# A hybrid decoder layer in fp32r passes: the output gate's inner product as fp32r products, and copies, low parts and loads moved between engines

## The chip, the cores and the metric

The kernel runs on one core of one Trainium2 chip. The metric is the time of one execution on the device, in microseconds (us); lower is better. Everything happens in a single launch: all weights come from the chip's memory (HBM), the result is written back to it, and the intermediate results that do not fit into SBUF go through HBM as well.

## The reference

One layer for a sequence of 1024 tokens and a model width of 1024, all in float32. What bears on the change:

```python
h = rms_norm(x) * (1 + sc1) + sh1
proj = h @ w_in                       # RG-LRU, RWKV-7 and attention branches, merge gates
lru_x, lru_y, p_rw, q, k, v, gates = jnp.split(proj, IN_POINTS, axis=-1)
# RWKV-7 branch: the output gate is a low-rank product over 160 inner channels
g = jax.nn.sigmoid(gl) @ g2           # gl: (1024, 160), g2: (160, 1024)
out = (y + bonus) * g                 # y: the delta-rule state's output
o_a = (ha * gelu(lru_y)) @ w_lru_o    # RG-LRU branch, 1280 inner channels
y_c = sliding_window_attention(q, k, v, q_gain, k_gain, sinks)
mixed = (gate_a * o_a + gate_b * o_b + gate_c * o_c) @ w_out
x = x + g1 * mixed
x = x + g2 * swiglu(rms_norm(x) * (1 + sc2) + sh2, w_ffn_in, w_ffn_out)
```

## The kernel before

**Layout.** Activations stand transposed in SBUF: 128 channels on the partitions, 1024 tokens along the free dimension. A dense product takes one block of 128 output channels at a time (`dense`, which calls `three_passes`). Both operands are split into a high part in fp32r and a low part, also fp32r, which is the value less its high part. A block is then, for every 128 input channels, three passes (high·high, high·low, low·high), each over two halves of 512 tokens: six matmul instructions of 128x512, all on line 250. The weight blocks form one stream with two slots: SyncE loads a block (`load_block`, line 232), GpSimd makes its high and low parts (`split_block`, lines 240 and 242), TensorE uses it. A slot is loaded again when its split is done, and split again when TensorE is done with it.

**No scheduler.** Each engine's program is written out by hand, one function per engine, with semaphores between them (`upto(n)` is a wait for the n-th event). What stands first in a function is done first; a wait in it holds back all that stands behind it on that engine. The DMAs that SyncE issues wait in the same way.

**The RWKV part** is a loop over 8 pairs of heads, 128 channels each, about 144 us a turn. A turn has six dense blocks (three of the branch, three of the merge gates). While block 3 runs, TensorE slips small work between its steps (`key_squares`): at steps 4 and 5 it makes the output gate's product for one half of the tokens each, `lg0` (128 inner channels, line 761) and `lg1` (32 inner channels, line 762), in plain float32. `g0` and `g1`, the gate's inner activations, are made once before the loop; the weights `lg0` and `lg1` are loaded for every pair. Behind the dense blocks come transposes to "tokens major" (line 784), four quarters of pair products (line 794), and then the inversion of a triangular matrix in six levels (lines 801 to 830). ScalarE (line 1316) and VectorE (line 1774) copy the transposed tiles out of PSUM, eight copies each; a quarter of the pair products waits for two copies more of either engine. VectorE masks each quarter's products (line 1777), and `v_am` releases TensorE to line 801.

**The attention part** runs in 32 ticks, 8 for each of 4 groups of heads. In a tick TensorE makes the scores of unit U (line 1004), turns the probabilities of unit U-2 (line 1017) and weighs the values of unit U-3 (line 1029). Between these it fills in dense work: in ticks 0 to 5 of a group the projection of the next group, and in the last group's ticks (24 to 31) the first four blocks of the next stage, `oa0` (`branch_part`). At tick 6 of a group `q_norms` makes 16 narrow products of two columns (line 988), whose sums ScalarE turns into a root (line 1428); group 0 has it ahead of tick 0. VectorE does the maxima (`peaks`, lines 1969 to 1978) and divisions (`divide`, lines 1984 to 1988), ScalarE the exponentials (line 1437) and the copies (lines 1445, 1453).

`oa0` needs four input tiles (k = 0 to 3) of the RG-LRU branch, `y_a`. SyncE loads them into three slots (`load_y`, line 586), ScalarE makes the high part (`high_y`, line 1463, in ticks 21 and 22), and VectorE the low part (`low_y`, line 1993, counted by `m_lo`, in ticks 22 and 23). The fourth tile goes into the first one's slot:

```python
sp.wait_ge(m_lo, upto(n - Y_SLOTS + 1))          # load_y
load_y(0, slice(0, 4))                           # all four, ahead of the first oa0 weights
...
pe.wait_ge(m_lo, upto(Y0[0] + k + 1))            # branch_part, line 1035 on
```

so on SyncE the first two weight blocks of `oa0` stand behind the wait of the fourth tile.

## Time and profile before

| what | value |
|---|---|
| median of 3 runs (lowest to highest) | 2959.48 us (2954.88 to 2963.72) |
| the profiled execution, and its span | 2960.99 us, 2959.2 us |
| TensorE matmuls busy | 2868.2 us, 97% |
| VectorE busy | 1426.8 us, 48% |
| ScalarE busy | 729.2 us, 25% |
| GpSimd busy | 710.6 us, 24% |
| mean granted TensorE clock | 0.994 of full speed |

The time is that of the whole launch, the span is the stretch from the first to the last instruction in the trace. A share of busy time is a mean over the whole program, over stages with different limits; where a single stage's time is asked for, it is read from rows of that stage. "PE" is TensorE, "DVE" VectorE, "ACT" ScalarE, "POOL" GpSimd, "SPq" the DMAs that SyncE issues. A float32 matmul leaves two records in the trace, an fp32r matmul one. Records of matmuls overlap, since they are pipelined, so the cost of one is the distance from its start to the next start.

### The profile page before, as it was taken

The numbers are of one execution on the slowest core, as the hardware profiler recorded it, in microseconds if no ns is written. First come the engines' busy times: TensorE is split into PE (matmuls) and PEld (weight loads), VectorE is DVE, ScalarE is ACT, GpSimd is POOL, SyncE is SP. The second block draws the span as 40 slices with busy tenths as digits, with TensorE's granted clock in tenths as the row PEclk, the third lists the DMA queues.
The fourth block names the chain that finished last, engine by engine and source line by source line (L and its number), as shares of the span: only waits on it lengthen the run. The fifth ranks groups of instructions, "written<-read, shape, count | busy, mean of one in ns | idle before, by whom it ended". The sixth has DMA issues, their size and how long they took to land.

```text
span 2959.2 us, 60581 instructions
## 1 busy us (share of the span) xinstructions
PE 2868.2 (97%) x25747; PEld 2352.8 (80%) x25747; DVE 1426.8 (48%) x1566; ACT 729.2 (25%) x1058; POOL 710.6 (24%) x454
## 2 busy tenths in 40 slices
PE   4999999999999999999999999999999999999999
PEld 4797979797978787877777776788887888888887
DVE  5645455455454545465654556476655222222223
ACT  3312121212131212145454666211122000000001
POOL 0302020303030202032222101333342333333332
PEclk9999999999999999999999999999999999999999
DMA  5211010202020201043331102376411111111112
GB/s 191 66 34 55 23 58 19 64 13 67 10 74 5 72 11 57 12 137 101 113 106 47 43 37 75 105 235 198 130 50 50 50 48 44 50 50 50 47 45 79
DMA packets 221843, 201.08 MB, mean 68 GB/s; under 512 B 22113, under 2 KB 192699, under 8 KB 221627
## 3 DMA queue, kind: packets, MB, share of 16 engines
q1 hardware_dynamic: 208160, 150.43, 17.2%
q10 hardware_dynamic: 13467, 47.31, 4.4%
q8 instruction: 191, 3.13, 0.5%
q14 instruction: 25, 0.20, 0.0%
HBM read 167.30 MB, written 30.41 MB: 67 GB/s over the span
## 4 chain that ended last, share of the span: by engine, by line
PE 94%; DVE 2%; issue 2%; DMA 1%; ACT 1%; SPq 0%; POOL 0%; ACTq 0%; POOLq 0%; DVEq 0%
PE ps L250 67%; PE ps L816 3%; PE ps L830 3%; PE ps L827 2%; PE ps L794 2%; PE ps L911 1%; PE ps L910 1%; PE ps L879 1%; PE ps L1004 1%; PE ps L784 1%; DMA arena<-in_w_ada 1%; PE ps L1029 1%; PE ps L1017 1%; PE ps L755 1%; PE ps L762 1%
## 5 line engine op out<-in xcount | busy, mean ns | idle before, releaser
L250 PE MATMUL ps<-x_hi,w_hi 128*128 128x512 f32 (+1 forms) x2576 | 836.0, 399 | 11.5 <-POOL w_lo L242 5.0
L250 PE MATMUL ps<-x_lo,w_hi 128*128 128x512 f32 (+1 forms) x2576 | 815.1, 391 | 0.0
L250 PE MATMUL ps<-x_hi,w_lo 128*128 128x512 f32 (+1 forms) x2576 | 814.8, 390 | 0.0
L240 POOL CAST w_hi<-w_raw 128x1024 fp32r<-128x1024 f32 (+2 forms) x221 | 211.8, 958 | 2199.5 <-PE ps L250 1628.6
L250 PEld LDWEIGHTS ps<-x_hi,w_hi 128*128 128x128 f32 (+1 forms) x2576 | 475.7, 188 | 144.3 <-issue 41.8
L250 PEld LDWEIGHTS ps<-x_hi,w_lo 128*128 128x128 f32 (+1 forms) x2576 | 483.4, 188 | 104.2
L250 PEld LDWEIGHTS ps<-x_lo,w_hi 128*128 128x128 f32 (+1 forms) x2576 | 483.7, 188 | 100.1
L242 POOL TENSOR_TENSOR w_lo<-w_raw,w_hi 128x1024 fp32r<-128x1024 f32 (+2 forms) x221 | 482.9, 2185 | 17.7
L2138 DVE TENSOR_TENSOR arena<-ps,arena 128x1024 f32<-128x1024 f32 x21 | 25.7, 1225 | 376.5 <-PE ps L250 376.5
L2156 DVE SCALAR_TENSOR_TENSOR arena<-ps,mod,arena 128x1024 f32<-128x1024 f32 x88 | 113.0, 1284 | 128.3 <-PE ps L250 128.2
L1800 DVE COPY_PREDICATED arena<-hid_lo,ps 128x256 f32<-128x256 int32 x144 | 72.0, 500 | 140.4 <-PE ps L827 89.4
L1586 ACT ACTIVATE hid_hi<-arena 128x1024 fp32r<-128x1024 f32 x22 | 23.4, 1062 | 442.0 <-PE ps L250 316.9
L250 PE MATMUL ps<-hid_hi,w_hi 128*128 128x512 f32 x352 | 109.0, 391 | 0.0
L250 PE MATMUL ps<-hid_hi,w_lo 128*128 128x512 f32 x352 | 108.5, 390 | 0.0
L250 PE MATMUL ps<-hid_lo,w_hi 128*128 128x512 f32 x352 | 108.5, 389 | 0.0
L1437 ACT ACTIVATE arena<-arena 128x256 f32<-128x256 f32 x128 | 75.4, 590 | 75.7 <-DVE arena L1978 75.7
L830 PE MATMUL ps<-arena 64*64 64x64 f32 x2560 | 89.9, 219 | 0.4 <-issue 0.4
L816 PE MATMUL ps<-arena 64*64 64x64 f32 x2560 | 84.8, 219 | 0.0
L830 PEld LDWEIGHTS ps<-arena 64*64 64x64 f32 x2560 | 83.5, 135 | 0.7 <-issue 0.6
L1767 DVE TENSOR_TENSOR arena<-ps,arena 128x1024 f32<-128x1024 f32 x8 | 9.8, 1224 | 151.0 <-PE ps L727 151.0
L816 PEld LDWEIGHTS ps<-arena 64*64 64x64 f32 x2560 | 80.3, 135 | 1.0
L1684 DVE TENSOR_TENSOR arena<-arena 128x1024 f32<-128x1024 f32 (+1 forms) x27 | 42.8, 1587 | 77.6 <-ACT arena L1266 76.4
(279 smaller groups left out, 3612.7 us busy)
## 6 DMA issues: line engine op xcount, KB each, us to landing
w_raw<-in_w_in SPq DMA_DIRECT2D x78, 512.0 KB, 4.0
arena<-in_w_ada SPq DMA_DIRECT2D x48, 512.0 KB, 4.6
w_raw<-in_w_ffn_in SPq DMA_DIRECT2D x44, 512.0 KB, 3.8
arena<-gates_sig ACTq DMA_DIRECT2D x40, 512.0 KB, 4.3
gates_sig<-arena ACTq DMA_DIRECT2D x24, 512.0 KB, 2.7
w_raw<-in_w_ffn_out SPq DMA_DIRECT2D x22, 512.0 KB, 3.5
arena<-in_x SPq DMA_DIRECT2D x16, 512.0 KB, 6.8
y_a<-arena ACTq DMA_DIRECT2D x10, 512.0 KB, 2.6
```

The source lines that it names most:

```text
L240: nc.gpsimd.tensor_copy(hi, raw).then_inc(s_whi, 1)
L242: nc.gpsimd.tensor_tensor(lo, raw, hi.bitcast(F32), ALU.subtract).then_inc(s_wsplit, 1)
L250: ins = nc.tensor.matmul(dst[h], wp, xp[h], start=first and m == 0, stop=last and m == 2)
L755: ins = mm(ps[hp, 4, c:c + 1], rw["bv"][hp, c * CHUNK:(c + 1) * CHUNK], ones[hp, 0:1], start=True, stop=True)
L794: ins = mm(dst, src[hp, c * CHUNK:(c + 1) * CHUNK], ar[hp, c, :, :], start=True, stop=True)
L816: ins = mm(bank(B, 2, hp)[:, c % BATCH, :], am[hp, c, AM_BA, :], xx[hp, 0, c, :], start=True, stop=True)
L827: ins = mm(bank(B, 0, hp)[:, c % BATCH, :], xx[hp, 1, c, :], y1[hp, c, :], start=True, stop=True)
L830: ins = mm(bank(B, 1, hp)[:, c % BATCH, :], y1[hp, c, :], xx[hp, 1, c, :], start=True, stop=True)
L1437: fn(sc[:, h, nn, :], sc[:, h, nn, :], ACT.Exp, bias=sm[:, SM_NEG, h, nn:nn + 1], scale=rq[:, gg % 2, t, n0 + nn, h:h + 1], accum_out=sm[: ...
L1684: v.tensor_tensor(dst, x0, x1, ALU.subtract).then_inc(v_mix, 1)
L1800: v.copy_predicated(blocks_of(xx[:, o, batch(B), :], lv, o), level_mask(lv, o), blocks_of(bank(B, o), lv, o)).then_inc(v_xu, 1)
L2156: v.scalar_tensor_tensor(r, ps[:, at:at + 2, :], mod[:, MOD_G2 + m:MOD_G2 + m + 1], r, ALU.mult, ALU.add).then_inc(m_dn, 1)
```

## The change

It has four parts.

1. **The output gate's product in fp32r.** The inner activations and the weights are split into high and low parts. For the 128-channel part the product becomes three fp32r passes. The 32-channel part is stacked on 96 partitions (activations high, low, high; weights high, high, low), so that one fp32r product with 96 rows gives all three. ScalarE and VectorE make the activations' parts once before the loop (two more steps on VectorE and three more copies on ScalarE, in the first pair's way); GpSimd makes the weights' parts in every pair, four small instructions behind the split of block 2; SyncE loads the 32-row weights three times. The masks move together in `hid`, and `g0`, `g1` leave the arena.
2. **Copies.** In the last quarter of the tokens-major copies ScalarE takes VectorE's two copies over (10 and 6 instead of 8 and 8).
3. **The narrow products.** `q_norms` is cut into two halves of 8; at tick 6 the second stands behind `weigh_values`, and each half waits for its own square alone.
4. **The first branch inputs.** The low parts of `oa0`'s four inputs are made by GpSimd, behind the splits of `oa0`'s first two blocks, and no longer by VectorE; SyncE issues the first two weight blocks of `oa0` ahead of the fourth input tile.

```diff
@@ build, the pair loop's layout
+        masks, g0_hi, g0_lo, g1_s = (hid[:, k * T:(k + 1) * T] for k in range(4))
+        lg0_hi, lg0_lo, lg1_s = (gate_w[:, k * P:(k + 1) * P] for k in range(3))
+        THIRDS = [slice(32 * k, 32 * k + 32) for k in range(3)]
+        G1_ROWS = slice(0, 96)
@@ SyncE
-                sp.dma_start(rw["lg1"][0:32, :], g2[P:160, bass.ds(i * P, P)]).then_inc(s_lw, 16)
+                for rows in THIRDS:
+                    sp.dma_start(rw["lg1"][rows, :], g2[P:160, bass.ds(i * P, P)]).then_inc(s_lw, 16)
...
-            load_y(0, slice(0, 4))
+            load_y(0, slice(0, Y_SLOTS))
...
                     load_block(sp, Block(nm, m % 2, m // 2), cols(wv, m * P, P), P)
+                    if g == 0 and m == 1:
+                        load_y(0, slice(Y_SLOTS, Y_POOL))
@@ GpSimd
                     split_block(pool, Block("rwkv", c, i), 1024)
+                    if c == 2:
+                        pool.wait_ge(s_lw, i * 96 + 96)
+                        pool.wait_ge(r_g, upto(i))
+                        wait_alone(pool)
+                        nc.gpsimd.tensor_copy(lg0_hi, rw["lg0"]).then_inc(l_split, 1)
+                        nc.gpsimd.tensor_copy(lg1_s[G1_ROWS, :], rw["lg1"][G1_ROWS, :]).then_inc(l_split, 1)
+                        pool.wait_ge(l_split, upto(i * 4 + 2))
+                        wait_alone(pool)
+                        nc.gpsimd.tensor_tensor(lg0_lo, rw["lg0"], lg0_hi.bitcast(F32), ALU.subtract).then_inc(l_split, 1)
...
+                        nc.gpsimd.tensor_tensor(lg1_s[low, :], rw["lg1"][low, :], lg1_s[low, :].bitcast(F32), ALU.subtract).then_inc(l_split, 1)
...
-            for nm, kts, *_ in BR:
+            for c in range(8):
+                split_block(pool, Block("oa0", c % 2, c // 2), BR[0][1] * P)
+                if c == 1:
+                    for k in range(Y_POOL):
+                        pool.wait_ge(m_hi, upto(k + 1))
+                        nc.gpsimd.tensor_tensor(x_lo[:, k, :], yraw[k % Y_SLOTS], x_hi[:, k, :].bitcast(F32), ALU.subtract).then_inc(y_low, 1)
+            for nm, kts, *_ in BR[1:]:
@@ TensorE
-                        mm(ps[:, 6 + h, :], rw["lg0"], rw["g0"][:, hs], start=True, stop=False)
-                        ins = mm(ps[:, 6 + h, :], rw["lg1"][0:32, :], rw["g1"][0:32, hs], start=False, stop=True)
+                        if h == 0:
+                            pe.wait_ge(a_wa, upto(6))
+                            pe.wait_ge(v_zero, upto(4))
+                            pe.wait_ge(l_split, upto(i * 4 + 4))
+                            wait_alone(pe)
+                        three_passes([ps[:, 6 + h, :]], (lg0_hi, lg0_lo), ([g0_hi[:, hs]], [g0_lo[:, hs]]), True, False)
+                        ins = mm(ps[:, 6 + h, :], lg1_s[G1_ROWS, :], g1_s[G1_ROWS, hs], start=False, stop=True)
...
-            def q_norms(gg):
-                pe.wait_ge(t_sq, upto(2 * gg + 2))
-                pe.wait_ge(t_k2, upto(2 * gg + 2))
+            def q_norms(gg, t):
+                pe.wait_ge(t_sq, upto(2 * gg + t + 1))
+                if t == 0:
+                    pe.wait_ge(t_k2, upto(2 * gg + 2))
...
-                pe.wait_ge(m_lo, upto(Y0[0] + k + 1))
+                pe.wait_ge(y_low, upto(k + 1))
@@ ScalarE
+                elif c == 1:
+                    fn(rw["A"], rw["A"], ACT.Sigmoid).then_inc(a_wa, 1)
+                    act.wait_ge(a_wa, upto(2))
+                    fn(g0_hi, rw["A"], ACT.Copy).then_inc(a_wa, 1)
                 else:
-                    t = rw["g0"] if c == 1 else rw["g1"][0:32, :]
+                    t = rw["t1"][THIRDS[0], :]
                     fn(t, t, ACT.Sigmoid).then_inc(a_wa, 1)
+                    act.wait_ge(a_wa, upto(4))
+                    for part in (0, 2):
+                        fn(g1_s[THIRDS[part], :], t, ACT.Copy).then_inc(a_wa, 1)
...
+                        if b0 == ALL_BY_ACT:
+                            for h, hp in enumerate(HEADS):
+                                src = ps[64:128, b0:b0 + 2, :].rearrange("p j (q h n) -> p j q h n", q=4, h=2)[:, :, :, h, :]
+                                fn(tk[hp, 2 * b0 + 1:2 * b0 + 4:2, :, :], src, ACT.Copy).then_inc(a_tk, 1)
@@ VectorE
+            dve.wait_ge(a_wa, upto(3))
+            v.tensor_tensor(g0_lo, rw["A"], g0_hi.bitcast(F32), ALU.subtract).then_inc(v_zero, 1)
+            dve.wait_ge(a_wa, upto(6))
+            v.tensor_tensor(g1_s[THIRDS[1], :], rw["t1"][THIRDS[0], :], g1_s[THIRDS[0], :].bitcast(F32), ALU.subtract).then_inc(v_zero, 1)
...
                     for b0 in (4 * B, 4 * B + 2):
+                        if b0 == ALL_BY_ACT:
+                            continue
...
-                if tick - 1 in Y_TICKS:
-                    for k in Y_TICKS[tick - 1]:
-                        low_y(0, k)
```

The order of the instructions at three places. On TensorE, inside block 3 of a pair (`ps` is PSUM, `x_hi` and the like the dense operands), before and then now:

```order
L250 MATMUL ps<-x_hi,w_lo 128x512 x2
L761 MATMUL ps<-arena 128x512
L762 MATMUL ps<-arena 128x512
L250 MATMUL ps<-x_hi,w_hi 128x512 x2
L250 MATMUL ps<-x_lo,w_hi 128x512 x2
L250 MATMUL ps<-x_hi,w_lo 128x512 x2
L761 MATMUL ps<-arena 128x512
L762 MATMUL ps<-arena 128x512
```

```order
L251 MATMUL ps<-x_hi,w_lo 128x512 x2
L803 ISA
L251 MATMUL ps<-hid,gate_w 128x512 x3
L806 MATMUL ps<-hid,gate_w 128x512
L251 MATMUL ps<-x_hi,w_hi 128x512 x2
L251 MATMUL ps<-x_lo,w_hi 128x512 x2
L251 MATMUL ps<-x_hi,w_lo 128x512 x2
L251 MATMUL ps<-hid,gate_w 128x512 x3
L806 MATMUL ps<-hid,gate_w 128x512
```

Two float32 products for each half of the tokens have become four fp32r ones at the same places, and one semaphore instruction (ISA) has come in.

On VectorE, between the transposes and the first mask of a pair (`arena` is the work memory in SBUF), before and then now:

```order
L1767 TENSOR_TENSOR arena<-ps,arena 128x1024
L1774 COPY arena<-ps 64x2x256 x8
L1776 ISA
L1777 TENSOR_TENSOR arena<-ps,hid_hi 128x1024
L1776 REGISTER_ALU
L1777 TENSOR_TENSOR arena<-ps,hid_hi 128x1024
```

```order
L1833 TENSOR_TENSOR arena<-ps,arena 128x1024
L1842 COPY arena<-ps 64x2x256 x6
L1844 ISA
L1845 TENSOR_TENSOR arena<-ps,hid 128x1024
L1844 REGISTER_ALU
L1845 TENSOR_TENSOR arena<-ps,hid 128x1024
```

Two copies fewer stand ahead of the first mask; they are now the last two of ScalarE's ten.

On SyncE, at the end of the attention's weights (`y_a` are the branch's inputs, `in_w_lru_o` the weights of `oa0`), before and then now:

```order
L232 DMA w_raw<-in_w_in 128x8x128 x2
L586 DMA arena<-y_a 128x1024 x4
L232 DMA w_raw<-in_w_lru_o 128x4x128 x2
L586 DMA arena<-y_a 128x1024
L232 DMA w_raw<-in_w_lru_o 128x4x128
```

```order
L233 DMA w_raw<-in_w_in 128x8x128 x2
L602 DMA arena<-y_a 128x1024 x3
L233 DMA w_raw<-in_w_lru_o 128x4x128 x2
L602 DMA arena<-y_a 128x1024 x2
L233 DMA w_raw<-in_w_lru_o 128x4x128
```

The fourth input tile has moved behind the first two weight blocks.

## Rows read from the trace of the kernel before

**Rows 1.** The page's part 4: the chain that ended last, by engine.

```profile
PE 94%; DVE 2%; issue 2%; DMA 1%; ACT 1%; SPq 0%; POOL 0%; ACTq 0%; POOLq 0%; DVEq 0%
```

**Rows 2.** Chain, pair 1, block 3 and after: start us, us, what.

```profile
281.17 0.86 PE ps L761 x2
...
283.07 1.60 PE ps L250 x6
...
286.58 13.83 PE ps L250 x60
...
316.42 0.93 PE ps L806 x32
```

**Rows 3.** Timeline, TensorE, gates of the RG-LRU branch: start us, us, what.

```profile
1284.00 1.13 PE L910 MATMUL ps<-arena 128*128 128x512 f32 x2
1285.06 1.12 PE L911 MATMUL ps<-arena 64*128 64x512 f32 x2
1286.11 1.13 PE L910 MATMUL ps<-arena 128*128 128x512 f32 x2
```

**Rows 4.** Timeline, pair 1: a low part on GpSimd, copies, pair products, masks.

```profile
290.81 2.40 POOL L242 TENSOR_TENSOR w_lo<-w_raw,w_hi 128x1024 fp32r<-128x1024 f32 x1
...
303.91 4.89 ACT L1316 ACTIVATE arena<-ps 64x512 f32<-64x512 f32 x8 [2.36 <-PE ps L784]
303.98 5.77 DVE L1774 COPY arena<-ps 64x512 f32<-64x512 f32 x8 [0.52 <-PE ps L784]
...
305.55 7.20 PE L794 MATMUL ps<-arena 64*64 64x128 f32 x128
...
309.78 2.36 DVE L1777 TENSOR_TENSOR arena<-ps,hid_hi 128x1024 f32<-128x1024 f32 x2
...
312.78 2.35 DVE L1777 TENSOR_TENSOR arena<-ps,hid_hi 128x1024 f32<-128x1024 f32 x2
...
315.27 1.15 PE L801 MATMUL ps<-arena 64*64 64x64 f32 x32 [0.65 <-DVE arena L1777]
```

**Rows 5.** The waits of TensorE: line waited for, us in total, times, longest.

```profile
PE ps L801 <- DVE arena L1777: 5.2, 8, 0.7
```

**Rows 6.** Timeline, TensorE, ticks 24 to 26 of the attention.

```profile
1795.06 1.13 PE L1004 MATMUL ps<-arena 64*128 64x256 f32 x8 [0.92 <-DVE arena L1969]
1801.02 0.79 PE L250 MATMUL ps<-x_hi,w_hi 128*128 128x512 f32 x1 [4.83 <-POOL w_lo L242]
...
1808.70 1.14 PE L1004 MATMUL ps<-arena 64*128 64x256 f32 x8
...
1814.84 1.14 PE L1004 MATMUL ps<-arena 64*128 64x256 f32 x8
```

**Rows 7.** Timeline of VectorE and ScalarE around tick 24.

```profile
1791.42 2.36 DVE L1993 TENSOR_TENSOR x_lo<-arena,x_hi 128x1024 fp32r<-128x1024 f32 x2
...
1796.17 1.06 ACT L1463 ACTIVATE x_hi<-arena 128x1024 fp32r<-128x1024 f32 x1 [4.22 <-DMA arena<-y_a]
...
1798.22 3.83 DVE L1993 TENSOR_TENSOR x_lo<-arena,x_hi 128x1024 fp32r<-128x1024 f32 x2
...
1800.98 1.00 ACT L1445 ACTIVATE arena<-ps 128x1024 f32<-128x1024 f32 x1
```

**Rows 8.** Windows, engines' busy time, granted clock (PEclk), DMA share, GB/s.

```profile
1588.00:1595.00 7.00, 7.00 (x31) 5.87 (x31) 1.58 (x2) 0.29 (x1) 0.15 (x1) 0.51 0.36 75
...
1801.00:1808.00 7.00, 6.98 (x34) 5.46 (x35) 5.37 (x9) 4.18 (x13) 2.80 (x2) 0.60 0.67 223
```

**Rows 9.** Timeline, TensorE, `q_norms` of group 0 and the first scores.

```profile
1586.30 5.30 PE L988 MATMUL ps<-keep,arena 128*128 128x2 f32 x32 [1.77 <-ACT arena L1403]
1591.53 2.08 PE L1004 MATMUL ps<-arena 64*128 64x256 f32 x8
```

**Rows 10.** Timeline of the first pair: ScalarE and TensorE.

```profile
124.37 1.06 ACT L1305 ACTIVATE arena<-arena 128x1024 f32<-128x1024 f32 x1 [3.65 <-DVE arena L1744]
...
128.39 0.63 PE L755 MATMUL ps<-keep,arena 64*64 64x1 f32 x16
```

More of the change, by code:

```diff
@@ L152, in build @@
         small = sb("small", [P, 96])
[L153 removed]
+        ARENA = 25344
         arena = sb("arena", [P, ARENA])
@@ L1118, in _ @@
                             pe.wait_ge(m_res, upto(half * 8 + i * 2 + c - 1))
-                        dense(pe, Block(f"wout{half}", c, i), tiles=HALF, first=first, ready=(m_lo, NY + HALF * half, 1))
+                        dense(pe, Block(f"wout{half}", c, i), tiles=HALF, first=first, ready=(m_lo, N_LOW + HALF * half, 1))
             def token_sums():
@@ L1153, in _ @@
             pe.wait_ge(m_res, upto(2 * KT - 1))
-            dense(pe, Block("ffn_first", 0), first=HALF, ready=(m_lo, NY + KT, 1), after=among_first)
+            dense(pe, Block("ffn_first", 0), first=HALF, ready=(m_lo, N_LOW + KT, 1), after=among_first)
             pe.wait_ge(m_res, upto(2 * KT))
```

72 lines of the change are left out of this document (44 added, 28 removed).

## The prediction, written before the run

> **What bounds the kernel now.** I read the page's chain first, then the waits of TensorE, then three timelines. The chain that ended last is 94% TensorE [rows 1]: the kernel is bound by the length of TensorE's own list, and whatever another engine gains counts only where TensorE waits for it. So I look for two things: TensorE work that gets shorter, and gaps on TensorE that close. The work is the gate's product [rows 2]. The gaps that the change touches are three: in every pair TensorE waits for VectorE's mask [rows 4, 5], at tick 24 of the attention for the split of `oa0`'s first weights [rows 6], and ahead of group 0's narrow products for ScalarE's square [rows 9]. The sum is made against the profiled execution's 2960.99 us; the median of the three runs, 2959.48, is 1.5 lower.
>
> **1. The gate's product, 19.4 us saved.** In block 3 a step of six fp32r matmuls with one half of the product takes from 283.07 to 286.58, 3.51 us [rows 2]. Sixty fp32r matmuls behind it take 13.83 us, so 0.2305 each and 1.38 for six. One half of the product therefore costs 3.51 - 1.38 = 2.13 us, of which the 128-row part's own 0.86 shows as a row [rows 2]; the remainder is the 32-row part and the change over to it and back. Two halves: 4.26 in a pair. Added are 8 fp32r matmuls, 8 x 0.2305 = 1.84. Net 4.26 - 1.84 = 2.42, times 8 pairs: **19.4 us**. All of it lies on TensorE's own list.
>
> The uncertain part is the product with 96 rows, a shape that the trace of before doesn't show. Where TensorE goes to a tile of 64 rows and back, four float32 records take 2.11 us (1284.00 to 1286.11) [rows 3], where two of full height take 0.86 and so four 1.72 [rows 2]: 0.39 more. If 96 rows cost that, each half is 0.39 dearer, 0.78 a pair and 6.2 in all, and the saving is 13.2. The other end is no extra. A saving below that, or a loss, has no reason: the four-fp32r-for-two-float32 exchange is of the same shapes as all other passes. I take no extra, since 96 rows fit in no half tile: the nearest row is the full 128-row tile of the dense passes themselves.
>
> The Trainium skill, "TensorE: Matmul & The Clock Gate", in its step-by-step part on loading weights, says that this load scales with the column count and that the row count doesn't matter. By that rule alone a tile of fewer rows would cost nothing extra and this part stays at 19.4; the row with the 64-row tile, which took 0.39 more, speaks against taking it that broadly.
>
> GpSimd makes the weights' parts behind the split of block 2. They start when block 0 is done and are asked for in block 3, two blocks later; a block is 48 matmuls of 0.2305, 11.1 us. Four instructions of an eighth of the size of one that takes 2.40 [rows 4] lie beside TensorE's work many times over; their price without that cover is rival (e). SyncE's two extra DMAs a pair are issued a whole pair ahead, behind the same wait as the other three.
>
> **2. The copies, 8.0 us saved.** VectorE's eight copies run 303.98 to 309.75, 0.72 each; then two masks (2.36), a scaling and two masks (2.35) up to 315.13; at 315.27 TensorE can go on [rows 4]. TensorE had been ready at some 314.45: its pair products end at 312.75 by their record, of which 0.16 is drain beside the next work, and two lots of 32 small products of 0.93 follow [rows 2, 4]. Recorded as waiting are only 0.65 a pair, 5.2 in 8 times [rows 5]; the rest of the 0.82 is booked as issue. With two copies fewer VectorE is 1.44 earlier, bound now by the last quarter's end at 312.75: last mask from 312.85 to 314.05, before TensorE's 314.45. So the wait goes wholly (0.82), and the masks of the inversion's first level, 1.08 earlier, release TensorE a further 0.2 sooner: **1.0 x 8 = 8.0 us**. Bounds: 5.2 (the recorded waits alone) and 8.4. Next late is ScalarE: ten copies of 0.61 from 303.91 end at 310.0, and the fourth quarter starts at 305.55 + 3 x 1.80 = 310.95 [rows 4]. The cover is 0.9 us; were it gone, TensorE would wait there instead.
>
> **3. Tick 24, 7.0 us saved.** From scores to scores an undisturbed tick takes 1814.84 - 1808.70 = 6.14 us, tick 24 takes 1808.70 - 1795.06 = 13.64 [rows 6]: 7.50 over, of which 4.83 is the wait for the low part of the weights. The rest is the clock: after that idle stretch the window from 1801 to 1808 shows a granted clock of 0.60 [rows 8], so most of it at the lower of the two levels, 1.2 GHz. The weights are late since SyncE issues them behind the wait for the first low part, which VectorE begins only at 1791.42 [rows 7]; that low part frees the slot for the fourth input. In the new order they are loaded and split as soon as the slots are free, long before. The 0.92 in front of tick 24's scores goes too, since VectorE's 2.36 of low parts stood ahead of that tick's maxima.
>
> What is late next: ScalarE waits 4.22 for the fourth input and ends its copy of the probabilities at 1801.98 [rows 7]; without that wait it ends at 1797.8, and TensorE turns those probabilities after two steps of `oa0`. With scores at 1794.1, done 1795.2, and 1.4 of `oa0`, TensorE is there at 1796.6 and waits 1.2. Tick 25 then begins at 1794.1 + 6.14 + 1.2 = 1801.5, not 1808.7: 7.2, and I take **7.0 us**. Bounds: 3.8 if the fourth input is as late as before (then the tick ends near 1804.9), and 8.4 (7.50 + 0.92) if nothing is late. GpSimd now makes four low parts here, 2.40 each as in [rows 4], while VectorE does its softmax.
>
> VectorE's pair of low parts took 3.83 beside GpSimd's splits, 2.36 otherwise [rows 7]. The Trainium skill, "SBUF — State Buffer", in "SBUF: two separate sides", says that a VectorE instruction with two SBUF inputs and a GpSimd one exclude each other for the instruction's whole length. The two rows agree with it. By that rule one division of VectorE may stand still for up to a whole low part, 2.4 us; the probabilities then come 1 to 2 us later and the sum for this part is 5 to 6.
>
> **4. The narrow products, 2.6 us saved.** In group 0 all 16 wait for the second square, 1.77 us, and then take to 1591.53 [rows 9], with the granted clock at 0.51 from 1588 on [rows 8]. Cut in two, the first half runs in the 1.77 us gap and the second from 1586.3; at the same pace (5.23 for both) it ends 1588.9, **2.6 us** earlier. Bounds: 0 (ScalarE's root and what follows set the start anyway) and 5.0 (the clock stays up as well: the scores behind them took 2.08 instead of 1.14 [rows 6, 9]). At tick 6 of the later groups I count nothing: the work is the same, and the clock's level there is as uncertain as in group 0.
>
> **5. The first pair, 0.8 us lost.** Ahead of the loop VectorE has two subtractions more and a wait for ScalarE's copies, 3 to 4.4 us later in all: two of 1.18 (half of 2.36 [rows 7]), and the rest an estimate for the wait, two copies of some 1 us as in 1.06 [rows 10]. Pair 0's prep hangs on it. ScalarE's square there ends at 125.43, TensorE needs it at 128.39 [rows 10]: 2.96 of cover. So 0 to 1.5 lost, I take **0.8**. In the other pairs nothing of this is there.
>
> Sum: 19.4 + 8.0 + 7.0 + 2.6 - 0.8 = 36.2. Against 2960.99: 2924.8; at the median's level **2923.3 us**, a ratio of 1.012.
>
> **The rivals.**
> (a) The 96-row product pays for the change of tile: 6.2 less saved, 2929.5. For it: every smaller tile in the trace pays. Against: none of those had more than 64 rows.
> (b) Tick 24's wait is replaced by another: fourth input or GpSimd's low parts late, 3.2 less, 2926.5. For it: four low parts in a row on GpSimd, 3.83 for two on VectorE under contention [rows 7]. Against: the input is asked for some 6 us earlier than before. The skill's exclusion rule, named above, is this rival's milder form, with part 3 at 5.5: 1.5 less, 2924.8.
> (c) The copies don't help: ScalarE's ten end after the fourth quarter wants them, cover 0.9. 8.0 less, 2931.3. Against: ten copies need a third longer than the rows say to get there.
> (d) The clock stays up at group 0's and tick 24's places: 2.4 + 1.4 more, 2919.5.
> (e) Slower than before: GpSimd's four weight parts in each pair hold back block 3's split, which stands behind them on its queue, and TensorE waits for it at each pair's block 3. It must cost more than 36.2 / 8 = 4.5 us a pair to make the kernel slower at all, 5.6 to make it 0.3% slower. Between the end of block 0 and the start of block 3 lie two blocks, 22.2 us; two splits of under 4 us each stand there already (the low part 2.40 [rows 4], the high part less), so TensorE waits once the four parts take more than some 15 us, and the kernel is slower from some 19 on. The rows' size for them is 1.5. At 21 us: 6 x 8 = 48 lost, 2971.
> (f) The product doesn't leave TensorE's path because the diff doesn't do what it says: the order of the instructions shows it at its place, so this has next to no chance.
>
> **How the numbers follow.** Forecast 0.42, (a) 0.22, (b) 0.12 and with (a) 0.05, (c) 0.04, (d) 0.10, (e) 0.02, others 0.03. The forecast's own unknown terms reach from 2918.3 (19.4 + 8.4 + 8.4 + 5.0, no loss: 41.2 saved) to 2938.8 (13.2 + 5.2 + 3.8 + 0 - 1.5 = 20.7 saved), both at the median's level, but not all at once. From (d)'s side to (a) and (b) together, 2932.7, with 3 us on either side for the scatter of a median: **2916 to 2936**, 8 in 10. About 0.3%, 9 us, is what a measurement of this kernel can tell from no change. Faster by more than that, 0.95; within it, 0.03; slower, 0.02.
>
> **What would show it.** In the profile of after: a step of block 3 with half a product takes 2.3 us instead of 3.51 (2.7 with (a)); no wait of the first-level products for the masks, the fourth quarter without a gap; the first `oa0` matmul within 0.3 us of tick 24's scores, and no window of half clock behind it; the first scores 2 to 3 us behind the square; in pair 0 a wait of 0 to 1.5 at the key sums. I am wrong if the step of block 3 stays above 3 us, if ScalarE becomes the releaser of the fourth quarter, or if GpSimd appears as a releaser of dense blocks in the pairs.

## The result, and where the 36 us went

| kernel | median (lowest to highest) | runs |
|---|---|---|
| before | 2961.7 us (2954.9 to 2966.9) | 9 |
| changed | 2943.3 us (2936.0 to 2949.1) | 9 |

The ratio of the changed kernel's time to that of before is 0.9939, with a 95% interval of 0.9928 to 0.995: 18 us faster, or 0.6%. The forecast was 2923.3, range 2916 to 2936: half of the saving is missing. The profiled execution of the changed kernel took 2944.2 us, its span is 2942.1 (before 2960.99 and 2959.2).

The page's chain is still TensorE's (93%, before 94% [rows 1]), so the missing part is time of TensorE again. Line numbers of the changed kernel: the dense passes are L251 (before L250), the key sums, small products that add up the squared keys, L794 (L755), the gate's half with 96 rows L806 (L761, L762), the pair products L838 (L794), the first level L845 and L850 (L801, L806), scores L1049 (L1004), the turning of the probabilities L1062 (L1017), the narrow products L1032 (L988).

First the places that went as forecast. The chain of pair 1 in the changed kernel; columns: start us, us, what.

```profile
286.12 2.28 PE ps L251 x9
288.40 0.23 PE ps L806
288.63 2.06 PE ps L251 x9
290.69 0.23 PE ps L806
290.92 13.62 PE ps L251 x60
...
309.75 7.13 PE ps L838 x128
316.88 0.93 PE ps L845 x32
317.81 0.93 PE ps L850 x32
318.75 0.93 PE ps L845 x32
```

The step with half a product takes 2.51 and 2.29 us where it took 3.51 [rows 2]; the record with 96 rows takes 0.23 like every other. The first level has two lots of products. Before, the second lot (315.27) stood still for VectorE's last mask [rows 4, 5]; now it follows the first without a gap (318.75), since that mask runs from 316.93 to 318.16 and nobody waits for it.

Then the list of TensorE's waits in the changed kernel; columns: line that waited, what it waited for, us in total, times, longest.

```profile
PE ps L1062 <- ACT arena L1505: 12.2, 6, 4.7
...
PE ps L794 <- ACT arena L1361: 5.5, 1, 5.5
```

The masks' line of [rows 5] is gone, the split of `oa0`'s weights too (it was the 4.83 of [rows 6]). In their place stand a wait of 5.5 us at the key sums of pair 0, and 12.2 for ScalarE's copy of the probabilities, 4.4 before; 6.5 of the 12.2 lie in ticks 22 to 24.

**Pair 0.** Timeline of VectorE in the changed kernel, then that of GpSimd in the same stretch; columns: start us, us, the instruction, in brackets the idle time before it and what ended it.

```profile
113.94 0.83 DVE L1804 COPY arena<-arena 128x16 f32<-128x16 f32 x1
...
115.01 2.25 DVE L1806 TENSOR_TENSOR arena<-arena 128x15 f32<-128x15 f32 x1
...
127.23 2.59 DVE L1810 TENSOR_SCALAR arena<-arena,rw_par 128x1024 f32<-128x1024 f32 x1 [0.16 <-DVE arena L1746]
```

```profile
113.37 1.36 POOL L241 CAST w_hi<-w_raw 128x1024 fp32r<-128x1024 f32 x1 [7.76 <-PE ps L251]
114.81 2.42 POOL L243 TENSOR_TENSOR w_lo<-w_raw,w_hi 128x1024 fp32r<-128x1024 f32 x1
124.25 1.74 POOL L241 CAST w_hi<-w_raw 128x1024 fp32r<-128x1024 f32 x1 [7.02 <-issue]
126.07 3.20 POOL L243 TENSOR_TENSOR w_lo<-w_raw,w_hi 128x1024 fp32r<-128x1024 f32 x1
```

The step on 15 columns (L1806) takes 2.25 us and ends at 117.26; GpSimd's low part of block 3 ends at 117.23. The copy ahead of it (L1804) takes 0.83 and ends with GpSimd's high part. Ten us later L1810 runs into the low part of block 4: 2.59 where it took 0.75. In the trace of before these two small steps took 0.18 each, and they ended before GpSimd began its split of block 3 at 116.38:

```profile
113.98 0.18 DVE L1740 TENSOR_TENSOR arena<-arena 128x15 f32<-128x15 f32 x1
...
123.58 0.75 DVE L1744 TENSOR_SCALAR arena<-arena,rw_par 128x1024 f32<-128x1024 f32 x1 [0.16 <-DVE arena L1686]
```

So ScalarE's square (L1361), at 124.37 before [rows 10], now starts at 129.85 although the whole pair began 3.0 us earlier. What TensorE does with that, from the chain:

```profile
129.85 1.07 ACT arena L1361
...
131.06 1.01 PE ps L794 x16
132.07 2.86 PE ps L251 x6
```

And the window behind the wait, in the changed kernel; columns: window, its length, busy us and instructions of TensorE, weight loads, VectorE, ScalarE and GpSimd, then the granted clock, DMA share, GB/s.

```profile
132.00:149.00 17.00, 17.00 (x83) 12.67 (x82) 10.15 (x11) 0.00 (x0) 0.00 (x0) 0.52 0.05 14
```

Six dense matmuls take 2.86 us instead of 1.38: the clock is at the lower of its two levels, 1.2 GHz, for nearly all of the 17 us behind an idle stretch of 5.5. From the pair's first lora product (L776, a low-rank product behind block 0, 100.12) to the first product behind its dense passes (L766, 163.96) it takes 63.8 us; pairs 1 to 7 take 50.6 each. **Pair 0 costs 13.3 us**, not 0.8.

**Ticks 22 to 24.** VectorE in tick 22, GpSimd and TensorE from there to tick 25, each from its timeline in the changed kernel.

```profile
1763.99 1.52 DVE L2042 SCALAR_TENSOR_TENSOR arena<-arena 128x4 f32<-128x4 f32 x1
1765.54 2.27 DVE L2044 TENSOR_TENSOR arena<-arena,nsinks 128x4 f32<-128x4 f32 x1
1767.84 0.16 DVE L2046 TENSOR_TENSOR arena<-small,arena 128x4 f32<-128x4 f32 x1
...
1775.45 1.22 DVE L2039 TENSOR_REDUCE arena<-arena 128x4 f32<-128x1024 f32 x1
...
1777.21 2.30 DVE L2044 TENSOR_TENSOR arena<-arena,nsinks 128x4 f32<-128x4 f32 x1
```

```profile
1763.12 4.66 POOL L702 TENSOR_TENSOR x_lo<-arena,x_hi 128x1024 fp32r<-128x1024 f32 x2 [0.61 <-ACT x_hi L1523]
1774.79 4.70 POOL L702 TENSOR_TENSOR x_lo<-arena,x_hi 128x1024 fp32r<-128x1024 f32 x2 [7.01 <-ACT x_hi L1523]
```

```profile
1760.29 1.13 PE L1049 MATMUL ps<-arena 64*128 64x256 f32 x8
...
1771.62 1.94 PE L1062 MATMUL ps<-keep,arena 128*128 128x128 f32 x8 [1.87 <-ACT arena L1505]
1775.56 1.51 PE L1049 MATMUL ps<-arena 64*128 64x256 f32 x8
1777.00 0.50 PE L251 MATMUL ps<-x_hi,w_hi 128*128 128x512 f32 x1
...
1783.33 1.94 PE L1062 MATMUL ps<-keep,arena 128*128 128x128 f32 x8 [4.66 <-ACT arena L1505]
1788.44 1.14 PE L1049 MATMUL ps<-arena 64*128 64x256 f32 x8
```

The first `oa0` matmul does follow tick 24's scores at once (1777.00), and ScalarE no longer waits for the fourth input. But GpSimd's low parts run in the middle of VectorE's softmax. The softmax steps on four columns, 0.16 us each otherwise, take 1.52 and 2.27 in tick 22 and 2.30 while TensorE is in tick 24. They end where GpSimd's instructions end: two low parts of 2.33 from 1763.12 end at 1765.45 and 1767.78, the steps at 1765.51 and 1767.81. A reduction (L2039, one input of 1024 columns) keeps its 1.22, though the one at 1775.45 begins inside the low part that runs from 1774.79. The exponentials are late by as much, and TensorE waits 1.87 and 4.66 for them, with half clock around. From the scores of tick 22 to those of tick 25: 28.15 us, before 27.72. TensorE's waits in this stretch are 6.5 us, before 5.7 (4.83 and 0.92). **Part 3 gives -0.4 us**, not 7.0.

The narrow products of group 0 and the first scores behind them, the answer to [rows 9]:

```profile
1563.93 3.88 PE L1032 MATMUL ps<-keep,arena 128*128 128x2 f32 x32
1567.74 1.73 PE L1049 MATMUL ps<-arena 64*128 64x256 f32 x8
```

From the end of the pairs to the first scores it is 339.0 us, before 342.3.

The budget, from the starts of the same lines in the two profiles:

| part | forecast | measured |
|---|---|---|
| gate's product, 8 x 2.41 | 19.4 | 19.3 |
| copies, 8 x 0.90 | 8.0 | 7.2 |
| ticks 22 to 24 | 7.0 | -0.4 |
| narrow products, group 0 | 2.6 | 3.3 |
| pair 0 | -0.8 | -13.3 |
| sum | 36.2 | 16.1 |
| start-up before pair 0 (103.1 to 100.1) | | 3.0 |
| solving stage, scatter over the pairs | | 4.2 |
| ticks 7 to 17, clock at other places | | -3.1 |
| behind the attention, 6.8 us at half clock | | -3.1 |
| all, and the difference of the spans | | 17.1 |

The start-up takes 100 to 104 us and a pair's solving stage 37.6 to 39.7 in all the profiles here, whatever the kernel; I count both as scatter. The last two losses aren't the change's either as far as the profiles tell: the kernel of experiment 3, whose attention and what follows it are those of before, shows both (tick 8 takes 12.64 us and tick 16 12.58, and 6.8 us at half clock stand behind the attention).

### The profile page after: what moved, and what is told of

It reads as the page before. It is cut to its first block, busy times and chain, and to the rows that moved or that the text cites. A ratio compares the mean times of both kernels' runs of the same rounds, so it can differ in the third digit from the quotient of the medians.

```text
span 2942.1 us, 60682 instructions
## 1 busy us (share of the span) xinstructions
PE 2850.9 (97%) x25747; PEld 2355.3 (80%) x25747; DVE 1423.2 (48%) x1549; ACT 742.4 (25%) x1077; POOL 750.5 (26%) x490
## 3 DMA queue, kind: packets, MB, share of 16 engines
q1 hardware_dynamic: 208928, 150.70, 17.2%
## 4 chain that ended last, share of the span: by engine, by line
PE 93%; DVE 3%; ACT 1%; issue 1%; DMA 1%; SPq 0%; ACTq 0%; POOL 0%; DVEq 0%; POOLq 0%
PE ps L251 67%; PE ps L860 3%; PE ps L874 3%; PE ps L871 2%; PE ps L838 2%; PE ps L955 1%; PE ps L954 1%; PE ps L923 1%; PE ps L1049 1%; PE ps L828 1%; DMA arena<-in_w_ada 1%; PE ps L1062 1%; PE ps L1074 1%; PE ps L794 1%; PE ps L880 1%
## 5 line engine op out<-in xcount | busy, mean ns | idle before, releaser
L251 PE MATMUL ps<-x_hi,w_hi 128*128 128x512 f32 (+1 forms) x2576 | 837.2, 399 | 7.4 <-issue 4.2
L251 PE MATMUL ps<-x_lo,w_hi 128*128 128x512 f32 (+1 forms) x2576 | 817.5, 392 | 0.0
L251 PE MATMUL ps<-x_hi,w_lo 128*128 128x512 f32 (+1 forms) x2576 | 816.8, 391 | 0.0
L251 PEld LDWEIGHTS ps<-x_hi,w_hi 128*128 128x128 f32 (+1 forms) x2576 | 478.7, 189 | 130.0 <-issue 31.0
L251 PEld LDWEIGHTS ps<-x_hi,w_lo 128*128 128x128 f32 (+1 forms) x2576 | 484.9, 188 | 105.2
L251 PEld LDWEIGHTS ps<-x_lo,w_hi 128*128 128x128 f32 (+1 forms) x2576 | 485.4, 188 | 101.3
L2203 DVE TENSOR_TENSOR arena<-ps,arena 128x1024 f32<-128x1024 f32 x21 | 25.7, 1225 | 376.4 <-PE ps L251 376.4
L251 PE MATMUL ps<-hid,w_hi 128*128 128x512 f32 x704 | 188.7, 390 | 0.0
L251 PEld LDWEIGHTS ps<-hid,w_hi 128*128 128x128 f32 x704 | 131.7, 188 | 27.1
L1868 DVE COPY_PREDICATED arena<-hid,ps 128x256 f32<-128x256 int32 x144 | 72.2, 501 | 138.1 <-PE ps L871 87.7
L1646 ACT ACTIVATE hid<-arena 128x1024 fp32r<-128x1024 f32 x22 | 23.4, 1064 | 442.0 <-PE ps L251 316.9
L251 PE MATMUL ps<-hid,w_lo 128*128 128x512 f32 x352 | 108.4, 389 | 0.0
L251 PEld LDWEIGHTS ps<-hid,w_lo 128*128 128x128 f32 x352 | 66.1, 188 | 13.8
```

The lines of the kernel that those rows point to most:

```text
L251: ins = nc.tensor.matmul(dst[h], wp, xp[h], start=first and m == 0, stop=last and m == 2)
L1868: v.copy_predicated(blocks_of(xx[:, o, batch(B), :], lv, o), level_mask(lv, o), blocks_of(bank(B, o), lv, o)).then_inc(v_xu, 1)
```

## The experiments

Diffs are against the changed kernel where nothing else is said. The theory: **a VectorE instruction that begins while one of GpSimd's is working in SBUF waits for that one's end**; the change pushed VectorE's chain in pair 0 onto GpSimd's splits, and put GpSimd's low parts onto VectorE's softmax. The rivals: the waits are chance of one profile; it is only the added work that makes VectorE late; it is the fourth input that is late. Line numbers differ a little from kernel to kernel. "Before" is the kernel before on the same chip: 2959.9 us for experiments 1, 2, 5 and 8, 2965.4 for 6, 7, 9 and 10, 2961.5 for 3, 4, 11 and 12. Ratios are to it.

**1. The gate's product alone** (gate_only). The copies, the narrow products and everything of part 3 as before.

```diff
-        ALL_BY_ACT = 6
+        ALL_BY_ACT = None
...
-            load_y(0, slice(0, Y_SLOTS))
+            load_y(0, slice(0, Y_POOL))
...
```

> The kernel before with the gate's product in fp32r alone (the copies, the narrow products and tick 24 as before). Theory (pair 0 pays for it): the steps of block 3 give 19.4 us over eight pairs, and pair 0 gives back 8 to 11, of which 5.5 is TensorE's wait at the key sums and the rest dense work at half the clock behind it; so 8 to 11 us faster than before, 2951 to 2953, and the key sums of pair 0 wait 4 to 6 us for ScalarE's square. Rival (pair 0's wait and the slow clock are an accident of one profile): 17 to 19 us faster, 2942 to 2944, with a wait under 1.5 us.

Measured: 2952.2 us, ratio 0.9973 (0.9962 to 0.9983), 8 faster. The wait at the key sums of pair 0 is there, 5.4 us. Block 3 is 2.41 us shorter in each of pairs 1 to 7. So pair 0's price belongs to the gate's product. That product brings work for VectorE and ScalarE ahead of the loop and weight parts for GpSimd in each pair; experiments 2 to 4 part them. One thing differs: the clock came back 6.8 us after it had fallen (0.90 in the window from 132 to 149), so pair 0 cost 7.5 here and not 13.3. This is one execution, the fastest of ten (2945.7 to 2958.6 us), so it does not say what pair 0 costs in the others.

**2. VectorE's small steps out of the way** (soft_early). The 26 steps of the decay rates (`e`, `z`, `acc`, `rate`, `rate2`) and two memsets move ahead of the first mixed stream; their input is ready by then.

```diff
+            e, z = rate2, small[:, 66:66 + LRU_T]
+            ...
             for c, (dst, width) in enumerate(((rw["wa"], P), (rw["A"], P), (rw["t1"][THIRDS[0], :], 32))):
                 mix_stream(c + 1, 2 * c, dst, ...)
-            e, z = rate2, small[:, 66:66 + LRU_T]
-            ...
```

> The changed kernel with VectorE's 26 small steps of the decay rates and its two memsets moved from in front of the pair loop to in front of the first mixed stream, where VectorE stands idle for 4.3 us. Theory (VectorE's chain in pair 0 comes too late and runs into GpSimd's splits): the wait of 5.5 us at the key sums of pair 0 is gone, the clock stays up there, and the kernel is 8 to 11 us faster than the changed one, 2932 to 2935. Rival (the clock falls in pair 0 whatever VectorE does): the wait goes but the half clock of some 20 us stays, 5 us faster, 2938. Second rival (the moved steps hold up the first streams by as much): 0 to 2 us.

Measured: 2934.4 us, ratio 0.9917 (0.99 to 0.9933), where the changed kernel has 0.9939 (0.9928 to 0.995). By the ratios that is some 6.5 us faster than the changed kernel, by the medians 8.9, and the intervals just touch, so the expected 8 to 11 are neither shown nor excluded in time. The profile is clearer. The wait is gone and so is the half clock; the same window of this kernel:

```profile
126.00:149.00 23.00, 23.00 (x153) 18.35 (x152) 10.71 (x9) 3.46 (x4) 6.85 (x4) 1.00 0.23 69
```

Pair 0 takes 25.26 us to its key sums and 25.31 from there, like every other pair; in the changed kernel 30.93 and 32.90. The slow clock went with the wait, and the first rival falls.

**3 and 4. Late on purpose** (late2, late4). The kernel before with two, or four, more clearings of a tile on VectorE ahead of the small steps. They do no work that is needed, and touch neither the gate nor GpSimd.

```diff
+            for k in range(4):
+                v.memset(rw["y1"], 0.0).then_inc(v_zero, 1)
+                dve.wait_ge(v_zero, upto(3 + k))
```

> The kernel before with two more clearings of a tile (0.91 us and some 0.1 of issue each) on VectorE in front of the decay rates' small steps, so that its chain into pair 0 is 2.1 us later and nothing else is touched. Both theories: cover 2.96, so no wait at the key sums of pair 0.

> The same with four clearings, 4.2 us later. If being late is the whole matter: a wait of 4.2 - 2.96 = 1.2 us at the key sums of pair 0. Theory (once late enough, the small steps begin inside GpSimd's low part of block 2 at 117.65 and wait for its end, and the tall ones meet the split of block 3): a wait of 3.5 to 6 us, and half clock behind it.

The lag is VectorE's scan (in before 111.22) minus TensorE's first lora product of pair 0 (in before 103.13). With four clearings, VectorE and then GpSimd, from their timelines, and TensorE's wait:

```profile
117.33 0.83 DVE L1742 COPY arena<-arena 128x16 f32<-128x16 f32 x1
...
118.41 2.25 DVE L1744 TENSOR_TENSOR arena<-arena 128x15 f32<-128x15 f32 x1
```

```profile
118.21 2.42 POOL L242 TENSOR_TENSOR w_lo<-w_raw,w_hi 128x1024 fp32r<-128x1024 f32 x1
```

```profile
PE ps L755 <- ACT arena L1305: 5.3, 1, 5.3
```

| kernel | lag of the scan | wait at the key sums | pair 0 over an undisturbed one |
|---|---|---|---|
| soft_early | 6.7 us | 0 | 0 |
| before | 8.1 | 0 | 0 |
| two clearings | 8.9 | 0 | 0 |
| four clearings | 11.2 | 5.3 | 13.0 |
| gate_only | 11.5 | 5.4 | 7.5 |
| changed | 11.5 | 5.5 | 13.3 |

The first two clearings cost little lag: 2.4 us of clearings, but the first of the small steps, which in before took 1.76 us beside a copy of GpSimd's, took 0.17 now. So the lateness was 0.8 and 3.1 where I had set 2.1 and 4.2. Against a cover of 2.96, four clearings are 3.1 late: by lateness alone TensorE would wait 0.1 us. It waits 5.3, with the same slow instructions as in the changed kernel, so the second expectation held. (It names the splits one block too low: GpSimd splits block 3 here and then block 4.) So the amount alone does not set the price; what stands where the chain arrives does: a step, not a slope. Between a lag of 8.9 and one of 11.2 nothing was measured, so where the step lies is open. The kernel with two clearings took 2959.3 us and the one with four 2977.8, one execution each, beside a median of 2961.5 for before.

**5. The low parts back on VectorE** (low_vector), the weights still ahead of the fourth input.

```diff
...
-                        nc.gpsimd.tensor_tensor(x_lo[:, k, :], yraw[k % Y_SLOTS], ...).then_inc(y_low, 1)
...
                 if nx < GROUPS and j == 6:
                     q_rsqrt(nx)
+                if tick - 1 in Y_TICKS:
+                    for k in Y_TICKS[tick - 1]:
+                        low_y(0, k)
```

> The changed kernel with the four low parts of the branch input made by VectorE at the ticks where it made them before; the weights stay ahead of the fourth input. Theory (the low parts on GpSimd hold back VectorE's small softmax steps for up to 2.3 us each, so the probabilities come late): TensorE's waits of 1.87 and 4.66 us for ScalarE's copy of the probabilities fall below 1.5 together, and the kernel is 5 to 8 us faster than the changed one, 2935 to 2938. Rival (it is the fourth input that is late, whoever makes the low parts): ScalarE's wait for it and TensorE's wait stay, within 2 us of the changed one. Second rival (VectorE has no room for its own 2.4 us pairs): slower by 1 to 3.

Measured: 2942.7 us, ratio 0.9943 (0.9927 to 0.996): nothing gained. My expectation fell, and the first rival was right about the place. Its VectorE and ScalarE, from the timelines:

```profile
1770.79 2.36 DVE L2057 TENSOR_TENSOR x_lo<-arena,x_hi 128x1024 fp32r<-128x1024 f32 x2
...
1775.57 0.16 DVE L2038 SCALAR_TENSOR_TENSOR arena<-arena 128x4 f32<-128x4 f32 x1
```

```profile
1775.50 1.06 ACT L1519 ACTIVATE x_hi<-arena 128x1024 fp32r<-128x1024 f32 x1 [4.19 <-DMA arena<-y_a]
```

The small steps are back at 0.16, as the theory has it. But the first low part starts at 1770.79, behind VectorE's reciprocal for the query norms, for which VectorE had stood idle 4.26 us. The fourth input is asked for only then, and ScalarE waits 4.19 for it ahead of the exponentials. TensorE waits 4.32 for the probabilities and 1.06 for VectorE's maxima, and the ticks 22 to 24 take 27.1. Two obstacles stood in the same place; taking one away uncovered the other.

**6. The first pair of low parts ahead of that reciprocal** (low_early). As 5, with two blocks of lines exchanged.

```diff
+                if tick - 1 in Y_TICKS:
+                    for k in Y_TICKS[tick - 1]:
+                        low_y(0, k)
                 if nx < GROUPS and j == 6:
                     q_rsqrt(nx)
-                if tick - 1 in Y_TICKS:
-                    ...
```

> The kernel of low_vector (low parts on VectorE, weights ahead of the fourth input) with the first two low parts in front of VectorE's reciprocal for the query norms in tick 22 instead of behind it; VectorE stands idle there for 4.3 us. Theory (low_vector gained nothing since its first low part came at 1770.8 us, so that the fourth input landed at 1775.4 and ScalarE waited 4.2 us for it ahead of the exponentials): the low parts come at 1766, the fourth input is there when ScalarE asks, TensorE's wait of 4.3 us for the probabilities falls under 1.5, and ticks 22 to 24 take 21 to 24 us instead of 27.1; 4 to 6 us faster than low_vector, 2937 to 2939. Rival (VectorE's second pair of low parts, or ScalarE's two table loads, hold the probabilities back just as long): under 1.5 us gained.

Measured: 2940.3 us, ratio 0.9912 (0.9894 to 0.993), where low_vector has 0.9943 (0.9927 to 0.996) on another chip; the intervals touch, so the forecast 4 to 6 us are neither shown nor excluded in time. ScalarE's copies of the third and fourth input follow each other, and TensorE's scores of ticks 22 and 25 stand 20.77 us apart:

```profile
1777.21 1.99 ACT L1519 ACTIVATE x_hi<-arena 128x1024 fp32r<-128x1024 f32 x2
```

```profile
1767.27 1.13 PE L1045 MATMUL ps<-arena 64*128 64x256 f32 x8
...
1779.11 1.13 PE L1045 MATMUL ps<-arena 64*128 64x256 f32 x8 [1.87 <-DVE arena L2033]
...
1784.43 1.06 PE L1058 MATMUL ps<-keep,arena 128*128 128x128 f32 x8 [2.60 <-ACT arena L1501]
...
1788.04 1.13 PE L1045 MATMUL ps<-arena 64*128 64x256 f32 x8
```

27.72 - 20.77 = 6.95 us: the size of the forecast's third part, but by luck and not by its terms. The wait for the probabilities fell from 4.3 to 2.6 and not under 1.5 as I had expected, and the wait for the maxima rose from 1.06 to 1.87. Both hang on VectorE's reciprocal for the query norms, which waits 2.01 us for ScalarE's root. Of the rival's two table loads (1.28 us each) the first stands in that chain; the second ends before VectorE's steps do. So the rival is right in part about the wait. Together TensorE waits 4.5 us, 5.4 in low_vector and 5.7 before. What shrank is its busy time in the three ticks, 16.2 us instead of 21.7 and 22.0. The granted clock is at the upper level through the whole stretch, where it is 0.75 in both others:

```profile
1767.00:1788.00 21.00, 16.46 (x142) 12.95 (x140) 16.88 (x29) 16.10 (x32) 1.90 (x2) 1.00 0.44 136
```

**7. GpSimd's low parts in quarters** (low_quarters). The changed kernel, each low part as four instructions of 256 columns.

```diff
-                        nc.gpsimd.tensor_tensor(x_lo[:, k, :], ...).then_inc(y_low, 1)
+                        for q in range(4):
+                            qs = slice(q * 256, (q + 1) * 256)
+                            ins = nc.gpsimd.tensor_tensor(x_lo[:, k, qs], ...)
+                        ins.then_inc(y_low, 1)
```

> The changed kernel with each of GpSimd's four low parts of the branch input cut into four instructions of 256 columns. Theory (a VectorE instruction that begins while GpSimd's is in SBUF waits until that one ends): VectorE's small softmax steps of ticks 22 and 24, which took 1.52, 2.27 and 2.30 us instead of 0.16, take 0.7 at most each; all of them together lose 1 to 2.5 us instead of some 6, and ticks 22 to 24 together take 25 to 27 us instead of 28.15. In time 1 to 3 us faster than the changed kernel. Rival (the slow small steps come from the engines' load as such, not from the length of GpSimd's instruction): they still take over 1.5 us each.

VectorE's softmax steps in tick 22 of this kernel:

```profile
1769.56 0.57 DVE L2045 SCALAR_TENSOR_TENSOR arena<-arena 128x4 f32<-128x4 f32 x1
1770.16 0.65 DVE L2047 TENSOR_TENSOR arena<-arena,nsinks 128x4 f32<-128x4 f32 x1
1770.85 0.65 DVE L2049 TENSOR_TENSOR arena<-small,arena 128x4 f32<-128x4 f32 x1
```

Where GpSimd's instruction is a quarter as long, VectorE's steps wait a quarter as long: 0.57 to 0.76 instead of 1.52 to 2.30, under the same load. The length of the other engine's instruction sets the wait; the rival falls. All steps on four columns together lose 3.0 us instead of 5.9 (I had said 1 to 2.5), TensorE waits 3.8 instead of 6.5, and ticks 22 to 24 take 24.65 us instead of 28.15. In time the gain can't be told from the changed kernel: 2942.7 us, ratio 0.9926 (0.9909 to 0.9942). This is the Trainium skill's rule in "SBUF — State Buffer", section "SBUF: two separate sides", that the port pair shared by VectorE and GpSimd is locked for a whole instruction; this trace agrees, down to the ends that meet within 0.1 us.

**8. The narrow products cut for group 0 alone** (norms_first).

```diff
-                if nx < GROUPS and j == 6:
-                    q_norms(nx, 0)
...
-                    q_norms(nx, 1)
+                    for t in range(2):
+                        q_norms(nx, t)
```

> The changed kernel with the narrow products cut in two for group 0 alone; at ticks 6, 14 and 22 all 16 stand together behind the turning of probabilities or the context, as before. Theory (the cut moves the fall of the clock from cheap stretches onto the tick's dense steps): ticks 8 to 9 and 15 to 17 take what they took before, 1.6 and 1.5 us less than in the changed kernel, so 2 to 4 us faster than it, 2939 to 2941. Rival (these ticks are long by chance of the clock): no difference beyond 1 us.

Measured: 2943.8 us, ratio 0.9946 (0.993 to 0.9963). Tick 8 takes 12.64 us and tick 16 takes 12.59, as in the changed kernel (12.63 and 12.55), where before took 11.00 and 9.75. My theory fell: the cut has no part in it. gate_only, in which nothing of the attention is touched, has 12.61 at tick 16 too, late2, whose attention is that of before, has 12.64 and 12.58, and the changed kernel's second profile has 9.84 at tick 16. These ticks are long or short by where the clock falls.

**9. The copies alone** (copies_only). Two copies a pair from VectorE to ScalarE in the kernel before.

```diff
+                        if b0 == ALL_BY_ACT:
+                            for h, hp in enumerate(HEADS):
+                                fn(tk[hp, 2 * b0 + 1:2 * b0 + 4:2, :, :], src, ACT.Copy).then_inc(a_tk, 1)
```

> The kernel before with ScalarE's two further copies a pair and nothing else. From the rows of the changed kernel each pair has 0.90 us less between the first two level products and the next ones: 7.2 us over eight pairs, and no pair 0 penalty, since VectorE's chain ahead of the loop is untouched: 2952 to 2954. Rival (the copies also help or harm pair 0): a difference of over 3 us from that.

Measured: 2955.6 us, ratio 0.9971 (0.9959 to 0.9982), which is 5 to 12 us faster than before (2965.4 on this chip; the 2952 to 2954 of the expectation are counted from a lower level, its 7.2 us are what compares). The profile has 0.90 us less in each of the eight pairs, 7.2 in all. Pair 0 has no wait.

**10 to 12. Both mends together,** twice, and the changed kernel again beside the second.

> Both mends together: the small steps of the decay rates ahead of the first stream (soft_early) and the low parts of low_early. If the two are independent: 2934.4 less 4 to 6, so 2928 to 2931, some 14 us faster than the changed kernel and 31 faster than the one before. If the place at tick 24 is held by something else: 2934, as soft_early.

> The changed kernel once more, on the same chip and beside the same runs of the kernel before as soft_low_again. It should stand at 0.992 to 0.995 of before, and its profile should again show 5.4 us of wait at the key sums of pair 0, and ticks 22 to 24 at 27 to 29 us together.

> Both mends once more, for the distance to the changed kernel on one chip: 12 to 16 us faster than it, ratio to before 0.987 to 0.990.

| kernel | median | ratio to before |
|---|---|---|
| soft_low | 2929.5 us | 0.9882 (0.9865 to 0.9898) |
| changed_again | 2942.3 | 0.9931 (0.9918 to 0.9943) |
| soft_low_again | 2925.1 | 0.9886 (0.9873 to 0.99) |

The changed kernel shows pair 0's wait (5.5 us) and ticks 22 to 24 (29.0) once more: they aren't chance. With both mends the kernel is 17.2 us faster than the changed one on the same chip, a little more than the 12 to 16 I had expected, and 36.4 faster than before. That is the size of the forecast's 36.2, but of another kernel: VectorE makes the low parts again, two blocks of its lines stand elsewhere, and the gain at tick 24 comes in good part with the clock. Ticks 22 to 24 take 22.3 us in the first profile and 20.8 in the second, and pair 0 has no wait in either.

## Why the prediction was wrong, step by step

**Step 1, the gate's product: right.** 2.41 us a pair against 2.42. Rival (a), that 96 rows pay, is out: the record takes 0.23, and its weight load 0.188 us as with 128 rows. Here the rule that the row count of a weight load doesn't matter (the Trainium skill, "TensorE: Matmul & The Clock Gate", section "Step-by-step: what each phase is for") and the trace agree; I had weighed it against the 64-row tile and kept its value. Rival (e) did not come: GpSimd appears in no wait of TensorE's in the pairs. In pair 0 its weight parts hold up four of VectorE's small steps by 0.5 us together.

**Step 2, the copies: right, a little large.** 0.90 a pair against 1.0: the wait of 0.82 went wholly, and of the further 0.2 only 0.08 came. Rival (c) is out: ScalarE's ten copies in pair 1 end at 314.17, 0.9 us before the fourth quarter starts, which is the cover of the forecast.

**Step 3, tick 24: failed.** The step was "what is late next". I followed ScalarE and the fourth input, and gave TensorE a wait of 1.2. The sentence "GpSimd now makes four low parts here, 2.40 each, while VectorE does its softmax" named the collision, but only a division of VectorE was set against it, 1 to 2 us, and only in a sentence beside the sum. Measured: the chain of small steps is stopped for 3.47 us in tick 22 and 2.45 in tick 24, one stop behind the other in the chain that ends in TensorE's wait of 4.66. A step of 0.16 us has no length of its own to price; it costs what is left of the other engine's instruction. Rival (b) had the right sign and the wrong cause in this kernel; its cause, the fourth input, showed up in experiment 5. The clock was the other half: the term took 2.7 us of half clock as gone with the wait, and it went wholly only in experiment 6, where TensorE still waits 4.5.

**Step 4, the narrow products: right in sign and size.** 3.3 against 2.6, within 0 to 5.0. From the cut at ticks 6, 14 and 22 I counted nothing, and experiment 8 finds nothing.

**Step 5, the first pair: failed, and it is the dearest.** VectorE was 3.4 us later against TensorE, inside the forecast's 3 to 4.4, but in part by luck: it came to its small steps 4.5 us later, then lost 1.6 less in the first of them, which in before had stood beside a copy of GpSimd's, and 0.5 more in others. The cover was 2.96. The step "so 0 to 1.5 lost" took the chain as a rigid thing that slides by 3.4. It slides onto GpSimd's splits of blocks 3 and 4 and grows by another 5.1 us (0.65 + 2.07 at the small steps, 0.54 + 1.84 at the tall ones), so the square is 8.5 late and TensorE waits 8.5 - 2.96 = 5.5; that wait is followed by 17 us at half clock, another 7.6 us. Both were there to be read: [rows 7] had VectorE's 3.83 for two low parts beside GpSimd, and [rows 6, 8] the half clock behind a wait of 4.83. I used both at tick 24 and neither at pair 0. The trace of before even had the case itself, small steps of VectorE's ahead of pair 0, 0.17 us each elsewhere, held up by GpSimd's split of block 2 (conversion from 103.36 to 104.40, then the low part):

```profile
103.41 1.02 DVE L1709 TENSOR_SCALAR lsc<-lsc 128x10 f32<-128x10 f32 x1
...
104.67 2.25 DVE L1709 TENSOR_SCALAR lsc<-lsc 128x10 f32<-128x10 f32 x1
```

```profile
104.49 2.40 POOL L242 TENSOR_TENSOR w_lo<-w_raw,w_hi 128x1024 fp32r<-128x1024 f32 x1
```

The range was too narrow for the same reason: its upper end, 2936, is rivals (a) and (b) together and 3 us of scatter, with pair 0 at 0.8, and even the outer bound of 2938.8 has it at 1.5. No rival had pair 0 for its place.

What stays open: why the clock came back after 6.8 us in the one profile of gate_only, where in every other profile with this wait pair 0 cost about 13. And 3.1 us in ticks 7 to 17 and 3.1 behind the attention belong to places where the clock fell in one profile and not in another. No experiment moved them on purpose.

## What to carry to other kernels

A cover is good only if the chain slides through free ground: before calling 3 us of delay hidden behind 3 us of cover, lay the shifted chain over GpSimd's timeline and see which instructions now meet. Work given to GpSimd beside a chain of VectorE's small steps cost here up to one whole GpSimd instruction (2.3 us) for a step, so either give it to VectorE in a gap that it has anyway, or cut it into short instructions (quarters brought a held-up step down to 0.6 to 0.8 us). When a stall of TensorE is removed or made, add the clock: here a wait of 5.5 us cost 13.

## What I hadn't expected of the hardware

- A VectorE copy of 16 columns with one input is held up too (0.83 instead of 0.18, until the end of GpSimd's conversion), and so is a one-input scale of 1024 columns (2.59 instead of 0.75; GpSimd's low part ends at 129.27 and the scale at 129.82). A reduction of 1024 columns isn't (1.22 from 1775.45, inside GpSimd's low part), nor is a clearing of 1024 columns (0.91 in late4 beside GpSimd's copy, 0.91 without it). The Trainium skill's "SBUF — State Buffer", section "Who interferes with whom", lists copies and scales among what can take the shared pair and reductions not; this trace agrees.
- Seven profiles with a wait of some 5.4 us on TensorE in pair 0 have 16.5 to 17.3 us of 1.2 GHz behind its end, one (gate_only) has 4.3. In the changed kernel TensorE was busy without a gap in that time (17.00 of 17.00 us).
- The same stretch of attention (ticks 8 and 16) took 11.0 or 12.6 us, and 9.8 or 12.6, in kernels that are alike there.
